# A hybrid encoder block: the order of four engines' work at the turn of a head pair and in its middle

## The reference, cut to what matters

```
cols = rms_norm(x) @ w_in          # q k v | r k v + LoRA-down | two merge gates
o_attn = banded_gqa_attention(q, k, v, sink)
o_rwkv = rwkv7_bidirectional(...)  # 32 heads of 64, scanned forward and backward
h = x + rms_norm((sigmoid(ga) * o_attn + sigmoid(gr) * o_rwkv) @ w_out)
out = h + rms_norm(relu(rms_norm(h) @ w_up) ** 2 @ w_down)
# inside rwkv7, per head and token, kk = normalised key:
kk = kk / max(sqrt(sum(kk * kk)), 1e-12)
S = S * w + (S @ -kk) (x) (kk * a) + v (x) k_mod ;  y = S @ r
```

## Time and profile before

| | us |
|---|---|
| median of 3 runs | 2294.17 |
| lowest, highest | 2293.75, 2302.84 |
| the profiled execution | 2292.01 |
| its span | 2290.2 |

### The profile page before, as it was taken

The page is one execution under the profiler, slowest core; times in us unless marked ns, Lnnn a source line. Parts: engine busy times, 40 slices in busy tenths (PEclk is TensorE's granted clock), DMA queues, the critical chain, the costliest instruction groups (busy, mean ns, idle before and its releaser), DMA issues.

```text
span 2290.2 us, 38980 instructions
## 1 busy us (share of the span) xinstructions
PE 2083.0 (91%) x14475; PEld 1897.0 (83%) x14475; DVE 1325.4 (58%) x2103; ACT 919.1 (40%) x1544; POOL 360.3 (16%) x424
## 2 busy tenths in 40 slices
PE   6999998998898988889988888879999999999996
PEld 6999998888888888888888766778988889889794
DVE  4766466766666666666666633455545545454454
ACT  4555333344444433344344423343434334343342
POOL 0000002333333333333333320000000000000000
PEclk9999999999999998999999858989999999999998
DMA  7555654322222222222230304535555655556552
GB/s 205 139 144 156 175 154 128 81 79 75 65 76 63 79 69 71 77 57 79 79 79 24 116 1 147 163 106 177 179 174 180 177 183 179 169 183 180 172 180 91
DMA packets 415085, 281.25 MB, mean 123 GB/s; under 512 B 14042, under 2 KB 372668, under 8 KB 414012
## 3 DMA queue, kind: packets, MB, share of 16 engines
q1 hardware_dynamic: 414620, 277.43, 41.9%
q10 hardware_dynamic: 416, 3.15, 0.3%
HBM read 278.46 MB, written 2.10 MB: 123 GB/s over the span
## 4 chain that ended last, share of the span: by engine, by line
issue 49%; PE 39%; ACT 4%; DVE 4%; POOL 3%; DMA 0%; SPq 0%; ACTq 0%; DVEq 0%; POOLq 0%
PE bank L1381 6%; PE bank L1382 6%; PE bank L1383 6%; PE bank L1589 3%; PE bank L1650 2%; PE bank L1655 2%; PE bank L1633 2%; PE bank L1397 1%; PE bank L1398 1%; PE bank L1399 1%; POOL AR L1315 1%; PE bank L1755 1%; POOL CT L1327 1%; POOL AR L1312 1%; ACT Dm L629 1%
## 5 line engine op out<-in xcount | busy, mean ns | idle before, releaser
L1381 PE MATMUL bank<-xT,whi 128*128 128x256 f32 x2784 | 833.6, 299 | 15.3 <-DVE wlo L772 6.7
L772 DVE TENSOR_TENSOR wlo<-raw,whi 128x2048 fp32r<-128x2048 f32 (+1 forms) x286 | 528.9, 1853 | 483.4 <-ACT whi L426 423.4
L1382 PE MATMUL bank<-xT,whi 128*128 128x256 f32 x2784 | 797.8, 287 | 0.0
L1383 PE MATMUL bank<-xT,wlo 128*128 128x256 f32 x2784 | 796.8, 286 | 0.0
L1381 PEld LDWEIGHTS bank<-xT,whi 128*128 128x128 f32 x2784 | 544.5, 196 | 20.4 <-issue 15.7
L1382 PEld LDWEIGHTS bank<-xT,whi 128*128 128x128 f32 x2784 | 545.0, 196 | 1.2
L1383 PEld LDWEIGHTS bank<-xT,wlo 128*128 128x128 f32 x2784 | 543.4, 195 | 0.0
L426 ACT ACTIVATE whi<-raw 128x2048 fp32r<-128x2048 f32 x166 | 316.9, 1909 | 288.8 <-PE bank L1399 288.8
L1397 PE MATMUL bank<-whi,ft 128*128 128x512 f32 x512 | 205.3, 401 | 12.3 <-PE bank L1399 9.3
L1398 PE MATMUL bank<-wlo,ft 128*128 128x512 f32 x512 | 202.2, 395 | 0.0
L1399 PE MATMUL bank<-whi,ft 128*128 128x512 f32 x512 | 202.1, 395 | 0.0
(11 more groups left out here) (211 smaller groups left out, 2918.2 us busy)
## 6 DMA issues: line engine op xcount, KB each, us to landing
raw<-in_w_in SPq DMA_DIRECT2D x106, 1024.0 KB, 5.9
raw<-in_w_ffn_up SPq DMA_DIRECT2D x64, 1024.0 KB, 6.3
raw<-in_w_ffn_down SPq DMA_DIRECT2D x64, 1024.0 KB, 5.0
raw<-in_w_out SPq DMA_DIRECT2D x16, 1024.0 KB, 5.1
raw<-in_w_in SPq DMA_DIRECT2D x4, 768.0 KB, 4.7
xtok<-in_x SPq DMA_DIRECT2D x2, 1024.0 KB, 5.7
upg<-in_g_up SPq DMA_DIRECT2D x16, 128.0 KB, 3.3
hres<-in_x ACTq DMA_DIRECT2D x1, 2048.0 KB, 9.1
```

Of the source, the lines that this page charges most:

```text
L772: x = V.tensor_tensor(wlo[:, u_static % 2, part], raw[:, u_static % 4, part], whi[:, u_static % 2, part].bitcast(f32), ALU.subtract)
L1381: M(bank[:, 0:T], h, xT[:, k, 0, :], start=k == 0, stop=False)
L1382: M(bank[:, 0:T], h, xT[:, k, 1, :], start=False, stop=False)
L1383: x = M(bank[:, 0:T], l, xT[:, k, 0, :], start=False, stop=k == KT - 1)
```

## The change

Four engines' orders are changed, and no instruction is added or removed.

1. ACT: the two copies into `Dm` go ahead of the wait for `y5`. The two half cuts `cut_pair(1, d1, d)`, which stood behind each of them, go behind the level-1 copy into `W` of the same direction. DVE: its two half cuts of that unit, of which the first stood at the head of the pair, go behind the level-1 writes of each direction.
2. PE: `heads(2)` and `heads(3)` go ahead of three dense steps, and `heads(2)` ahead of the gate's product, `heads(3)` ahead of the bonus.
3. Key norm: ACT squares ahead of `decays_exp`; PE sums behind L1713, ahead of `lora_a`; DVE clamps ahead of the scans and spreads ahead of the half cut and of `Sm`; PE turns it ahead of the state product.

```diff
@@ ACT pair @@
+                for d in range(2):
+                    w("d0p", d + 1)
+                    A.activation(Dm[:, :, 2 * d:2 * d + 2, :], PB[4 - d][:, :].rearrange(...), ACT.Copy)\
+                        .then_inc(s["d0"].sem, 1)
                 act.wait_ge(s["y5"].sem, s["y5"].before(i))
                 w("lg")
                 w("bonv")
                 A.activation(gup[:], ...)
                 A.activation(gt[:], ...)
-                for d in range(2):
-                    w("d0p", d + 1)
-                    A.activation(Dm[:, :, 2 * d:2 * d + 2, :], ...)
-                    cut_pair(1, d1, d)
...
                         A.activation(W[d][:]...)
+                        if l == 1:
+                            cut_pair(1, d1, d)
...
                     if c == 0:
                         if n is not None:
+                            squares(n)
                             decays_exp(n)
                         cut_pair(3, d1, 0)
                         if n is not None:
                             rates(n)
-                            squares(n)
@@ DVE pair @@
-                cut_pair(1, d1, 0)
...
-                        if l == 1 and d == 0:
-                            cut_pair(1, d1, 1)
+                        if l == 1:
+                            cut_pair(1, d1, d)
...
                     if nx and c == 0:
+                        nx.keys()
                         nx.products(0)
                         nx.products(1)
...
                         if nx:
-                            nx.keys()
+                            nx.norm()
                         cut_pair(3, d1, 0)
                         w("smm")
...
-                        if nx:
-                            nx.norm()
@@ PE pair @@
                     inc(x, "resm")
                     if nx and c == 0:
+                        nx.squares()
                         w("kbs2")
                         nx.lora_a()
...
                     if c == 0:
-                        if nx:
-                            nx.squares()
                         w("due", c + 1)
+                        if nx:
+                            nx.norms()
...
                         dense(c, d2, 12, KT)
-                        if nx:
-                            nx.norms()
...
                 if gram:
+                    gram.heads(2)
+                    gram.gate()
+                    gram.heads(3)
+                    gram.bonus()
                     dense(2, d2, 0, EARLY // 2)
-                    gram.gate()
-                    gram.heads(2)
-                    gram.bonus()
-                    gram.heads(3)
```

More of the change, by code:

```diff
@@ L621, in pair @@
                 w = lambda name, k=None: act.wait_ge(s[name].sem, s[name].at(i, k))
+                for d in range(2):
+                    w("d0p", d + 1)
+                    A.activation(Dm[:, :, 2 * d:2 * d + 2, :], PB[4 - d][:, :].rearrange("p (d h c) -> p d h c", d=2, h=2), ACT.Copy)\
+                        .then_inc(s["d0"].sem, 1)
                 act.wait_ge(s["y5"].sem, s["y5"].before(i))
@@ L626, in pair @@
                 A.activation(gt[:], raw4[:, 3, 1:T + 1], ACT.Tanh, scale=0.5).then_inc(s["gate_t"].sem, 1)
-                for d in range(2):
-                    w("d0p", d + 1)
-                    A.activation(Dm[:, :, 2 * d:2 * d + 2, :], PB[4 - d][:, :].rearrange("p (d h c) -> p d h c", d=2, h=2), ACT.Copy)\
-                        .then_inc(s["d0"].sem, 1)
-                    cut_pair(1, d1, d)
                 for l in range(1, LV):
@@ L1727, in pair @@
                     if c == 0:
+                        w("due", c + 1)
                         if nx:
-                            nx.squares()
-                        w("due", c + 1)
+                            nx.norms()
                         w("kbs2")
```

## The result

The changed kernel takes 2271.6 us (median of 4 runs, 2260.4 to 2275.3) against 2298.4 us on the same chip; the ratio is 0.9875, 95% interval [0.9831, 0.992]. It is faster, by 1.25% and not by the 3% that was forecast, and its runs lie 15 us apart. Its profiled execution is the fastest of them, 2260.4 us. Medians and ranges are of fast runs; one slow run, of e10, is left out.

A forecast was written before the change was run, and what follows sets the result against it. In the recurrent mixer PE is busy nine tenths of the time, so only its idle time and clock could give. Turns 51, middles 13, pair 0 −1.2, last pairs +0.5 and +1.0: 65 off 2292.0, 2227 us; range 2208 to 2258.

The forecast's parts named there:

- That the clock holds is my choice between two ends.: In the turn, PE's clock was taken to stay at full rate, with 0.3 us more gained per turn on average.
- control: Stretches of the kernel before, with single PE idles of 1.36 us (first pair) and 2.10 us, where the clock held.
- (a): Rival, chance 0.13: the clock still falls in the turn after several idle times within 7 us, 2.6 per turn; 2268 us.
- (c): Rival, chance 0.03: the clock falls later, at two new stalls before level 3, with 10.2 us of half rate; 2302 us.
- (b): Rival, chance 0.10: the middle gives nothing, as POOL's power or ACT's rates hold PE ahead of the state product; 2240 us.
- (d): Rival, chance 0.04 with anything unseen: Dm copies ahead of the gate are inert, as W still stands behind it; near 2290 us.
- Walk of part 1: In the turn, Dm copies ahead of the gate and later cuts of unit 3 were to gain 3.5 us.
- Part 2: Third and fourth Gram sets ahead of filler on PE: a cost of 0.14 us per turn, ends 0 and 0.3.
- Part 3: Key norm earlier in the middle: power taken as 1.96 us, gain 0.95; the other end, power 1.02, gain 1.3.
- The period without a fall: Sign that the forecast is right: a period from pair to pair near 58.0 us.
- Pair 0: Its turn has no fall and no gate to gain from, only the later cuts: about 1.2 us longer.

The follow-up runs named there:

- e10: The changed kernel with the Gram sets put back in the old order; 2271.1 us, ratio 0.9889 to the kernel before.
- e9: The changed kernel plus nine products nobody reads, on PE in the 1.27 us wait ahead of level 2, d=1; 2228.6 us, ratio 0.9688.
- e2: The kernel before with only the copies into Dm and the half cuts of unit 3 moved; 2277.4 us, ratio 0.9923.
- e1: The changed kernel with both halves of unit 3's cut moved on ACT and DVE into the pair before; 2200.6 us, ratio 0.9585.
- e5: e1 with PE's product of the variance's root moved ahead of three dense steps; 2179.7 us, ratio 0.9494.
- e3: The kernel before with only the key norm's squares, sums, clamp, spread and product moved earlier; 2290.8 us, ratio 0.9975.
- e7: The changed kernel with only ACT's half cuts of unit 3 moved to the pair before, DVE's left in level 1; 2229.0 us, ratio 0.9701.

## Why the prediction was wrong

The direction, the place and the dependencies were right; the time lay outside the range because one choice, on the clock, failed.

- **The step that failed: "That the clock holds is my choice between two ends."** It held in only 5 of the loop's 14 periods. The falls cost (60.10 − 57.89) × 14 = 31 us, of a miss of 33 in the profiled execution (65 forecast, 31.6 measured). e9 gives the same size from the other side: its loop is 31 us shorter (the medians lie 43 apart, as the changed kernel's profiled execution is its fastest). The argument for the choice compared single idle times ("the longest idle is 1.05 us, against 1.36 and 2.10 without a fall"). The measured turn has no longer one than 1.27 and falls all the same, in some passes and not in others that are identical up to it. Neither control had three waits close together, and each was a single passage: the changed kernel's turn, too, passes without a fall 5 times in 14. The two controls even lie 5.4 us apart, in the same passage of the kernel before (timeline of PE, the first below; the second in the earlier trace rows), 3.46 us of idle time without a fall where the changed turn has 2.86. So the sum of idle time alone doesn't say when the clock falls.

```profile
393.80 0.36 PE L1381 MATMUL bank<-xT,whi 128*128 128x256 f32 x1 [2.10 <-DVE wlo L772]
```

- **Rivals (a) and (c)** each had a part of it. (a), with 0.13, named the reason, several idle times within 7 us, and its 2268 is near the measured 2272 (profiled 2260). It took the price of the old falls, 2.6 us, for every turn; measured are 2.2 on average, from nine turns in 14. That the total comes near is in part luck. (c), with 0.03, named the place, the new stalls and not the old ones. It was priced as if every turn had 10.2 us of half rate. A stretch of 6.8 us cost 2.2 to 2.6 us, one of 10.2 cost 4.1 to 4.4, not quite the half that was assumed. (b) and (d) did not come: PE's wait for rep is gone, and so is the one for Dm, with W's down to 1.03.
- **Walk of part 1: right but for the half cut.** From the first L1632 to that of level 3, d=0 it gave 8.49 us; measured 8.98. The difference is the half cut at 1.77 and not 1.23 beside POOL, which moved the stall ahead of level 2 from 0.8 to 1.27; of the next one, 0.85 in the walk, 0.28 is left. W and L1649 came 2.23 behind the first L1632, as walked.
- **Part 2: right to the size of what can be read.** A cost of 0.14 was given, e10 shows a gain of 0.06.
- **Part 3: the end not taken was the right one.** POOL's power took 1.09 beside the scans and not 1.96; rep took 0.35 and PE had no wait. e2's periods against the changed kernel's give 1.5 us per middle, the forecast had 0.95 and an upper end of 1.3. The rule of the Trainium skill ("GPSIMD Engine Reference", 1. Specifications: contention with VectorE instructions that have two SBUF inputs) doesn't come out here: the scans do have two, and the power beside them took 1.09, near the 1.02 beside a masked copy. The measurement decides. The rule does agree for DVE's half cut, which stretched to 1.77 beside POOL.
- **The period without a fall**, 57.89, was forecast as 58.0. That it is so near is in part luck: the middle gained 0.55 us more than forecast, and the turn lost 0.49 more.
- **Pair 0:** expected 1.2 longer; from its second copy into Dm to KB it took 24.36 us against 19.78. In e9, where the clock holds there, it takes 21.36: so 1.6 is the cuts and 3.0 the fall again, a half-rate stretch of 7 us. The first copy into Dm came another 1.7 later (398.32 against 396.67), and the cause of that was not looked for.

Open: what decides, between two turns alike to 0.04 us, in which one the clock falls. It was not tried apart.

## What to carry to other kernels

A wait of PE has two prices, its own length and the half rate that may follow it, and only the first shows in a list of waits. So look at all the idle time close around a new wait, and not at the longest piece. Don't take one passage without a fall as proof that the clock holds: the same code fell in 9 turns of 14. When a fall can't be ruled out, give it a real share of the chances. Filling such a wait with work that nobody reads is a cheap test of that price, and here a better kernel. When an instruction is moved off the path, read who waits for its *last* half: the way out was to put the cuts about 17 us earlier (e1), where PE waits for neither half.

## What the runs showed of the hardware that was not expected

- The clock falls behind waits of PE of 0.56, 1.03 and 1.27 us within 8 us in 9 of 14 turns of the same code; with the last one filled with products, in none (e9); with a single wait of 0.99 us, in none (e5).
- Adding 126 products to the loop (6203 against 6077 in the windows) made it 31 us shorter (810.2 against 841.3).
- With some 1.5 us saved elsewhere in the period, the half-rate stretches were longer, 154 us together and not 116 (e3).
- DVE's subtraction of a half cut took 1.22 us, 1.50 (e7) or 1.77 by what POOL ran beside it; POOL's power took 1.09 beside scans and 1.96 beside such a cut. In the overlaps of such a cut with POOL in the turn shown, the one that started second took longer than elsewhere: the cut at 523.00 (1.77) behind AS (522.24 to 523.68), the mask at 523.63 (1.66, against 0.68 at 521.61) behind that cut.
